# Moved products, turns and value products at the starts and ends of two attention layers, with the input loaded by column quarters

## The reference

```python
# layer 0: 16 heads of 64 in 4 groups; proj = x @ w_in holds q, and k, v of three branches, and gates
s_c = q @ k_cmp.T; p_c = softmax(s_c, masked)      # k_cmp, v_cmp: 31 blocks, gelu(blocks @ w1 + b1) @ w2
o_s, o_w = causal softmax attention on rotated q   # the selected-block and the window branch
out = (g0 * p_c @ v_cmp + g1 * o_s + g2 * o_w) @ w_o
# layer 1: logits = q @ k.T * scale + cum_q - cum_k, cum = cumsum(log_sigmoid(fl + b_f))
out = (causal_softmax(logits) @ v) @ w_o
# both:  x = layer_norm(alpha * x + out);  h = causal_conv3(x @ w_up) + b
#        x = layer_norm(alpha * x + (gelu(h_a) * h_b) @ w_down)
```

## Time and profile before

| | |
|---|---|
| time, median of 3 runs | 1358.13 us (1357.21 to 1358.55) |
| profiled execution, its own time | 1358.98 us |
| its span | 1357.2 us |
| mean granted TensorE clock | 0.994 |
| busy: PE, DVE, ACT, POOL | 1320.9, 633.8, 678.0, 604.1 us |

### The profile page before, as it was taken

The page is one execution under the profiler, slowest core; times in us unless marked ns, Lnnn a source line. Parts: engine busy times, 40 slices in busy tenths (PEclk is TensorE's granted clock), DMA queues, the critical chain, the costliest instruction groups (busy, mean ns, idle before and its releaser), DMA issues.

```text
span 1357.2 us, 19897 instructions
## 1 busy us (share of the span) xinstructions
PE 1320.9 (97%) x6872; PEld 1109.6 (82%) x6872; DVE 633.8 (47%) x1478; ACT 678.0 (50%) x1261; POOL 604.1 (45%) x401
## 2 busy tenths in 40 slices
PE   9989999989999999999999999998999999999997
PEld 6878888877888888888889788886898888888886
DVE  4357777782644434430015667768354333441005
ACT  4457777774444444441225777776244444443122
POOL 2458686763244444444434222332344444444442
PEclk9989999999999999999999999999999999999999
DMA  9633232224233333334323412312433333334321
GB/s 293 138 86 79 70 79 79 71 55 143 76 93 98 104 93 93 93 93 145 102 79 96 102 48 65 80 64 66 152 94 109 93 104 96 93 100 133 99 72 63
DMA packets 172798, 131.98 MB, mean 97 GB/s; under 512 B 24544, under 2 KB 156244, under 8 KB 172724
## 3 DMA queue, kind: packets, MB, share of 16 engines
q1 hardware_dynamic: 172724, 131.02, 33.4%
HBM read 117.17 MB, written 4.39 MB: 90 GB/s over the span
## 4 chain that ended last, share of the span: by engine, by line
PE 89%; DVE 4%; ACT 3%; issue 2%; POOL 1%; DMA 0%; SPq 0%; DVEq 0%; ACTq 0%; POOLq 0%
PE ps L1007 16%; PE ps L1008 16%; PE ps L1009 16%; PE ps L1275 7%; PE ps L1274 7%; PE ps L1277 7%; PE ps L1162 3%; PE ps L1134 2%; PE ps L1176 2%; PE ps L1326 2%; PE ps L1322 2%; PE ps L1321 2%; PE ps L1175 1%; PE ps L1086 1%; PE ps L1265 1%
## 5 line engine op out<-in xcount | busy, mean ns | idle before, releaser
L512 POOL TENSOR_TENSOR wl<-raw,wh 128x1024 fp32r<-128x1024 f32 x178 | 427.1, 2403 | 646.6 <-ACT wh L639 646.5
L1007 PE MATMUL ps<-xh,wh 128*128 128x512 f32 x960 | 378.9, 395 | 5.0 <-ACT qf L714 3.6
L1008 PE MATMUL ps<-xl,wh 128*128 128x512 f32 x960 | 375.6, 391 | 0.0
L1009 PE MATMUL ps<-xh,wl 128*128 128x512 f32 x960 | 375.3, 391 | 0.0
L639 ACT ACTIVATE wh<-raw 128x1024 fp32r<-128x1024 f32 x192 | 201.1, 1050 | 198.2 <-PE ps L1277 184.6
L1007 PEld LDWEIGHTS ps<-xh,wh 128*128 128x128 f32 x960 | 181.1, 189 | 42.1 <-ACT qf L714 4.5
L1009 PEld LDWEIGHTS ps<-xh,wl 128*128 128x128 f32 x960 | 181.0, 189 | 38.6
L1008 PEld LDWEIGHTS ps<-xl,wh 128*128 128x128 f32 x960 | 181.1, 189 | 33.1
L1794 DVE SCALAR_TENSOR_TENSOR work<-ps,conv,work 128x511 f32<-128x511 f32 x88 | 66.0, 749 | 222.0 <-ACT work L874 156.1
L734 ACT ACTIVATE prob<-prob,negmax 128x128 f32<-128x128 f32 x192 | 107.4, 559 | 56.2 <-DVE negmax L1559 54.0
L1275 PE MATMUL ps<-wl,gh 128*128 128x512 f32 x344 | 135.2, 393 | 0.0
(11 more groups left out here) (233 smaller groups left out, 1970.3 us busy)
## 6 DMA issues: line engine op xcount, KB each, us to landing
raw<-in_ffn_w_up SPq DMA_DIRECT2D x88, 512.0 KB, 3.8
raw<-in_ffn_w_down SPq DMA_DIRECT2D x44, 512.0 KB, 3.5
raw<-in_fox_w_in SPq DMA_DIRECT2D x24, 512.0 KB, 4.1
raw<-in_nsa_w_in SPq DMA_DIRECT2D x12, 512.0 KB, 5.0
xt<-in_x SPq DMA_DIRECT2D x8, 512.0 KB, 5.0
raw<-in_nsa_w_in SPq DMA_DIRECT2D x16, 256.0 KB, 3.7
qs<-work SPq DMA_DIRECT2D x32, 128.0 KB, 2.3
raw<-in_nsa_w_o SPq DMA_DIRECT2D x8, 512.0 KB, 3.6
```

The costliest lines, as they stand in the source:

```text
L512: nc.gpsimd.tensor_tensor(wl[:, slot, :, :], raw[:, slot, :, :], wh[:, slot, :, :].bitcast(F32), ALU.subtract).then_inc(s_wl, 1)
L1007: nc.tensor.matmul(o, ah, bh, start=start, stop=False)
L1008: nc.tensor.matmul(o, ah, bl, start=False, stop=False)
L1009: return nc.tensor.matmul(o, al, bh, start=False, stop=stop)
```

## The change

1. x is loaded by column quarters (all 512 rows, 256 columns), with chunk 0 behind the first. PE turns two blocks k a quarter and puts chunk 0's products by its high part between the quarters; ACT and DVE split x block by block.
2. Ahead of the NSA loop, PE's order becomes: compressed scores, scores of units 0 and 1, the values' turn, `conv_turn`, compressed values. DVE takes the first two maxima before the compressed softmax; ACT loads the table for the exponential earlier; the split of the compressed values goes into units 1 to 4, chunk 9 into unit 0 (ACT) and, in thirds, 1 to 3 (POOL).
3. The compressed branch's two products a head become one, with both parts side by side as weights.
4. From unit 99 on, NSA's value products stand one unit later (even u, before the turn); in FoX all do.
5. The second tile's products for k = 0 to 3 (eight of three products each) go between the last turns and value products of both attentions (`second_tile`), and `down_pe` starts with tiles 2 and 3. FOX_EARLY is repacked: `first_tile` (2, 0) at v = 2 and (3, 0) at v = 3.
6. Small tiles are put together.

```diff
-FOX_EARLY = {1: (0, 0), 2: (1, 0), 3: (0, 1), 4: (1, 1), 5: (2, 0), 6: (2, 1), 7: (3, 0)}
+NSA_LATE_PV = NSA_UNITS - 29
+FOX_EARLY = {0: [(0, 0)], 1: [(1, 0)], 2: [(2, 0)], 3: [(0, 1), (3, 0)], 4: [(1, 1)], 5: [(2, 1), (3, 1)]}
+SECOND_TILE = {-2: [(0, 0), (1, 0)], -1: [(2, 0), (3, 0)], 0: [(0, 1), (1, 1), (2, 1), (3, 1)]}
...
-            for c in range(3):
+            for q in range(QT):
+                cs = slice(q * 2 * P, (q + 1) * 2 * P)
+                sp.dma_start(xt[:, :, cs], t["x"][0][:, cs].rearrange("(m p) c -> p m c", p=P)).then_inc(s_xn[q], 16)
+                if q == 0:
+                    sp.dma_start(small[0][0], small[0][1]).then_inc(s_ld[0], 16)
+                    load(0, 0, cols(w_nsa, D))
+            for c in range(1, 3):
...
+            for k in range(KB):
+                act.wait_ge(s_xt, k + 1)
+                nc.scalar.activation(xh[:, k, :], ps[:, 1 + k % 7, :], ACT.Copy).then_inc(s_xh, 1)
+                if k == 1:
+                    hi(0, 0)
...
             cmp_gelu(1)
+            load_table(ACT.Exp)
             item_hi(0, 1)
             item_copy(0, 2)
...
+            unit_exp(0, 0)
+            unit_exp(1, 1)
+            cmp_exp(0)
             item_hi(0, 2)
...
+            for q in range(QT):
+                pe.wait_ge(s_xn[q], 16)
+                block_turn(2 * q)
+                block_turn(2 * q + 1)
+                if q == 0:
+                    keep_warm(6, BP)
+                else:
+                    by_high_part(0, 0, BP, 2 * q - 2)
+                    by_high_part(0, 0, BP, 2 * q - 1)
+            by_high_part(0, 0, BP, KB - 2)
+            by_high_part(0, 0, BP, KB - 1)
+            by_low_part(0, 0, BP)
...
                 if p % 4 == 1:
+                    if p == 1:
+                        pe.wait_ge(s_cmpr, 2)
                     pe.wait_ge(s_cl, H // 2 + 1)
-                    for part in range(2):
-                        nc.tensor.matmul(ps[0:HD, bank, :], vcs[:, part, H % 2, g, :], pcs[:, :], start=False, stop=False)
+                    nc.tensor.matmul(ps[:, bank, :], vcs[:, H % 2, g, :, :].rearrange("p a d -> p (a d)"), pcs[:, :], start=False, stop=False)
...
+            def second_tile(c0, oh, ol, left, units):
+
+                pe.wait_ge(s_nm, units - 1 if left else units)
+                for k, h in SECOND_TILE[left]:
+                    down_half(c0 + k, k, 1, h, oh, ol, OUT_AT, k == 0, False)
...
             item_steps(2)
+            pe.wait_ge(s_cmpr, 1)
+            cmp_scores(0)
+            pe.wait_ge(s_ge, 4)
+            nsa_scores(0)
+            nsa_scores(1)
+            values_turn(0, BO)
+            conv_turn(1, BT + 1)
             pe.wait_ge(s_gel, 2)
...
+                    if u >= NSA_UNITS - 2:
+                        second_tile(C_WO0, oh, ol, u - NSA_UNITS, NSA_UNITS)
...
-                    if u % 2 and u >= 3:
+                    if u % 2 and 3 <= u < NSA_LATE_PV:
                         nsa_pv((u - 3) // 2)
+                    if u % 2 == 0 and u >= NSA_LATE_PV:
+                        nsa_pv((u - 4) // 2)
...
+            nsa_pv(NSA_UNITS // 2 - 2)
+            second_tile(C_WO0, oh, ol, 0, NSA_UNITS)
             nsa_pv(NSA_UNITS // 2 - 1)
...
-                down_pe(c0, KB, n, oh, ol, OUT_AT, range(1, QT), bank_ready, block_ready, (0, 2), range(1, QT))
+                down_pe(c0, KB, n, oh, ol, OUT_AT, range(2, QT), bank_ready, block_ready, (0, 2), range(2, QT))
...
-                        first_tile(C_WO1, oh2, ol2, HEADS, *FOX_EARLY[v])
-                    if v % 2 and (v > 1 or not first):
-                        fox_pv((U + v - 3) // 2)
+                        for at in FOX_EARLY[v]:
+                            first_tile(C_WO1, oh2, ol2, HEADS, *at)
+                    else:
+                        second_tile(C_WO1, oh2, ol2, v - 8, NSA_UNITS + FOX_UNITS)
+                    if v % 2 == 0 and (v > 2 or not first):
+                        fox_pv((U + v - 4) // 2)
                     turn(U + v, v % 4)
...
             fox_stages(7, 1, None, more=False)
-            first_tile(C_WO1, oh2, ol2, HEADS, 3, 1)
+            fox_pv((NSA_UNITS + FOX_UNITS) // 2 - 2)
+            second_tile(C_WO1, oh2, ol2, 0, NSA_UNITS + FOX_UNITS)
             fox_pv((NSA_UNITS + FOX_UNITS) // 2 - 1)
...
             cmp_mask(0)
...
             unit_max(0, 0)
             unit_max(1, 1)
             unit_inverse(0)
+            cmp_difference(0)
+            conv_copy(1, BT + 1)
...
                         item_dve(g, 2)
+                    if u == 0:
+                        cmp_sum(0)
+                        cmp_inverse(0)
+                        cmp_gate(0)
+                    if u in (3, 4):
+                        cmp_values_lo(range(2 * (u - 3), 2 * (u - 2)))
```

## The result

The changed kernel took 1353.12 us (median of 8 runs, 1350.96 to 1354.36), the kernel before 1359.47 in the same series; the ratio is 0.995, with a 95% interval from 0.9938 to 0.9961, which is 5.3 to 8.4 us; by the two medians it is 6.4. The profiled execution took 1353.09, its span is 1351.3 against 1357.2 before: 5.9 us less. In a second series of runs the ratio was 0.9961 (0.9949 to 0.9973).

A forecast was written before the change was run, and what follows sets the result against it. PE was taken as the bound, busy 1320.9 of 1357.2 us. Terms 1.9 + 3.9 + 2.1 + 3.0 + 1.8 - 3.1 - 2.6 = 7.0 us off 1358.1 gave 1351.1, range 1344.5 to 1355.5.

The forecast's parts named there:

- The start: Loading x by quarters, chunk 0 second in the queue: chunk 0 ends near 16.7, gain 1.9 us, bounds 0 and 3.
- the loop's start: Ahead of the NSA loop: PE's gaps shrink, gain 3.9 us, and the lower clock behind them goes, gain 2.1.
- the compressed product: One compressed product in place of two, 32 become 16 at 0.23 us each where PE is full: gain 3.0.
- the end of NSA: Later value products gain 0.7 us; second-tile products at the end net 1.1 after 1.4 lost cover: gain 1.8.
- FoX's steady pairs: FoX before its last pair: PE has k-steps throughout, so moving value products changes nothing, 0 us.
- the end of FoX: FoX's last pair: waits for POOL's low parts and lost cover cost 3.1 us, the lower clock 2.6.
- rival D: At the start, the quarters of x gain nothing: 1353.0 us; chance 0.05.
- The low end: For the single compressed product, a gain of 1.5 us if the loop is held elsewhere.
- Rival C: Gap ahead of the NSA loop only half closed, DVE's moved work holding units 0 to 5: 1354.3 us; chance 0.14.
- A: At FoX's end the waits come but the clock stays at 2.4 GHz: 1348.5 us; chance 0.18.
- B: FoX's low parts are in time because ACT reaches chunks 2 and 3 sooner: 1342.0 us; chance 0.10.
- E: Slower: FoX's lower clock, once called, stays through the output products up to about 985, 1373 us at 45 us; chance 0.06.

The follow-up runs named there:

- by the experiment: Changed kernel with the value products of FoX's pairs 0 to 6 back at the odd units, last pair as changed: 1357.28 us, ratio 0.9992.
- the second trace of the changed kernel: The changed kernel run and profiled once more without edits, against the kernel before: 1353.03 us, ratio 0.9961.
- The experiment shows: Changed kernel with first-tile products of FoX's last pair reordered, (2,0) and (2,1) at v = 4, (3,0) and (3,1) at v = 5: 1344.4 us, ratio 0.9896.

## Why the prediction was right, and where it was not

The total was near (1351.1 predicted, 1353.1 measured; a gain of 7.0 predicted, 5.9 found by the trace and 6.4 by the medians), and that is luck in good part. The start, the loop's start, the compressed product and the end of NSA gave 7.2 us where 12.7 were predicted, 5.5 too few; FoX's steady pairs and the two feed-forward parts gave 4.4 that were not predicted at all. What was right in its mechanism are the two largest terms, the start of the loop and the end of FoX. Point by point:

**The start (1.9 predicted, 0.2 found)** failed at the step "with chunk 0 second in the queue, quarter four lands at about 11.8", and in what was hung on it. The fourth quarter landed at 12.6, but PE came to its transposes only at 13.25, so it held nothing up. The second quarter set the time: it came behind chunk 0 and landed at 9.5, and PE's work from there, 8.7 us, was never summed up. What I took for the end of the chain (the last thing to land) was not it. The sign set for rival D, a first chunk that ends at 18 or later, came (18.2), and with it D's outcome for this term.

**The start of the loop (6.0 predicted, 5.6 found)** was right in its parts: the 0.90 of waiting, put down to the queries' transfer, and the full clock up to unit 5. "No PE gap over 1 us from 70 to 90" was missed by one, the 1.17 for `qf`. The price of what had moved into units 0 to 5 was 1.17 in place of 0.5, and it fell at one place, ACT's copy of the item, at 89.6. With the loop's start undone 6.2 arrives at the end. Rival C did not come.

**The compressed product (3.0 predicted, 0.9 found).** The step that failed is "0.23 each where PE is full". The single product takes 0.29 at its place, so it saves 0.19, and PE was not the bound there: behind the product stands a turn that waits for POOL. The low end named the condition ("if the loop is held elsewhere"), but the loop was taken to be full from the share of PE's busy time and not read unit by unit.

**The end of NSA (1.8 predicted, 0.5 found).** The end itself came as worked out: the last value products end at 314.0 in the changed kernel, 319.6 in times of before (5.6 are from earlier), where 320.0 was forecast; the wait for `ol` is 1.35, where 1.4 was. The "0.7, bounds 0 and 2" for the value products moved from unit 99 on was of the wrong sign: they were the cover of the wait for head 14's queries, and without them the two waits and the half clock cost 2.3 to 2.4. A step was moved past a DMA's wait, and I had not named the work that hid it.

**FoX's steady pairs (0 predicted, 2.4 found).** "Moving value products changes nothing" failed. The line to see was PE's wait for `work` from ACT L927, 1.0 us in six, too small for the list of the earlier trace rows; it costs 0.28 a pair, 2.0 in all by the experiment. The other 0.4 stays open.

**The end of FoX (-5.7 predicted, -5.8 found).** Both waits were forecast (3.3 and 3.6; found 3.01 and 2.85), and so was the lower clock. Its price was put at 2.6. By the windows it is 5.61 us of busy time at 0.50 and 4.00 at 0.59, so 2.8 and 1.6, 4.4 in all; the waits, 1.0 shorter than forecast, make up for a part of it, and 0.7 isn't traced. That the number fits so well is luck: the second trace of the changed kernel has waits of 3.01 and 3.63, the lower clock only behind the second, and -5.0. The experiment shows that 7.6 to 8.2 us were to be had here. Rivals A, B and E did not come: the clock fell, the low parts were late, and the full clock was back from 934.

**Not predicted at all:** 1.0 us in each feed-forward part, whose code is the same (last section).

## What to carry to other kernels

Before a step is moved, ask what each wait behind it was covered by: 0.5 us of value products were the cover of a DMA's landing, and without them the gap also took the clock down, and it cost 2.4 in all. Work put into a gap must have its operands by then: read the release time of every operand from the trace, since a product whose weights come 3 us later turns the filler into the stall. And a saved instruction pays only where its engine doesn't wait within the next unit; compare two traces unit by unit, and a gain that falls back one unit later shows at once where the loop is held.

## What the runs showed of the hardware

**The clock can fall after shorter gaps than the one read before, and doesn't always.** In the first trace of the changed kernel PE ran at 1.2 GHz behind both waits for `wl`, 3.01 and 2.85 us. In its second trace the first wait was as long and the clock stayed; it fell behind the second, 3.63. That trace, timeline and window:

```profile
921.39 0.50 PE L1014 MATMUL ps<-wh,oh 128*128 128x512 f32 x1 [3.01 <-POOL wl L512]
928.14 0.80 PE L1014 MATMUL ps<-wh,oh 128*128 128x512 f32 x1 [3.63 <-POOL wl L512]
```
```profile
920.00:927.00 7.00, 3.11 (x19) 2.51 (x19) 3.90 (x8) 2.83 (x7) 2.59 (x2) 0.99 0.24 75
```

Of ten traces with this first wait (3.01 to 3.03), six show the lower clock behind it and four don't, and the end of FoX costs from 4.6 to 6.7 us in them. In NSA's last group, behind the waits of 0.58 and 1.76 us with 0.4 us of work between, it was low in all nine traces that have them. In the trace with two compressed products the start's wait for x was 2.66, and the clock stood at 0.57 from 12 to 15; in the changed kernel the same wait was 2.07 and the clock stayed. First the one, then the other:

```profile
12.00:15.00 3.00, 3.00 (x13) 2.70 (x12) 1.49 (x3) 1.19 (x2) 0.00 (x0) 0.57 1.01 235
```
```profile
12.00:15.00 3.00, 3.00 (x21) 2.46 (x19) 1.97 (x4) 2.20 (x5) 0.00 (x0) 1.00 1.06 247
```

The spread of a transfer's landing (0.2 us of start, 9.78 against 9.58) thus became 1.8 us at the end of chunk 0. So with a wait of 2.7 us or more, as here, the clock behind it is to be priced as a chance and not as a fixed sum.

**A weight load of 128 columns** took 0.192 us and one of 64 columns 0.137, both for the compressed product (line L1219 of the changed kernel, L1193 of the one before). The single product's successor starts 0.29 after it; in the k-steps, whose loads have 128 columns too, it is 0.23, so the width of the load alone doesn't explain the 0.06. The Trainium skill (TensorE: Matmul & The Clock Gate, "LDWEIGHTS (loading the stationary operand)") has a load's time go in proportion to its columns. By these two durations it rises with them, but by 1.4 for twice the columns.

**Two rates of the same product.** In the down projections the kernel before has 229 ns between products of 512 columns where all the others have 227, with the same operations and the clock at 1.00 in both. Lines of the stretch from 640 to 700, first of the kernel before, then of the changed one (busy us, mean ns):

```profile
L1275 PE MATMUL ps<-wl,gh 128*128 128x512 f32 x88 | 34.6, 393 | 0.0
L1274 PE MATMUL ps<-wh,gh 128*128 128x512 f32 x88 | 34.3, 390 | 0.0
```
```profile
L1312 PE MATMUL ps<-wl,gh 128*128 128x512 f32 x89 | 34.6, 389 | 0.0
L1311 PE MATMUL ps<-wh,gh 128*128 128x512 f32 x89 | 34.6, 389 | 0.0
```

It makes 2.0 of the 5.9 us. The change merges small tiles and so moves the places of others in memory, which may be the cause; no run separates that from a property of the one execution that was profiled, so it stays open.
